# A decoder step whose mixture-of-experts loop takes experts 4 to 15 in an order worked out on the chip

## What is computed

```python
def moe_tokens(x, w_router, r_bias, wg, wu, wd):
    T = x.shape[0]
    scores = jax.nn.sigmoid(jnp.einsum('td,de->te', x, w_router, preferred_element_type=jnp.float32))
    ...
    h = jax.nn.silu(jnp.einsum('td,edf->tef', x, wg)) * jnp.einsum('td,edf->tef', x, wu)
    h = h * combine[..., None].astype(h.dtype)
    return jnp.einsum('tef,efd->td', h, wd)
```

## Time and profile before

| | us |
|---|---|
| median of 3 runs | 1412.61 (1407.36 to 1415.7) |
| the profiled execution | 1414.74 |
| its span | 1413.1 |
| TensorE, matmuls | 1206.3 busy, 85% of the span |
| VectorE | 463.3, 33% |
| ScalarE | 259.4, 18% |
| GpSimd | 157.0, 11% |
| chain that ended last | PE 68%, DMA 13%, DVE 10%, issue 4% |

### The profile page before, as it was taken

How to read it: one execution, slowest core, us unless ns; L and a number is a source line. 1 busy time by engine, 2 the same in 40 slices (tenths; PEclk the granted TensorE clock), 3 DMA queues, 4 the chain that set the end, 5 groups by cost and what they waited for, 6 DMA issues and landing times.

```text
span 1413.1 us, 26886 instructions
## 1 busy us (share of the span) xinstructions
PE 1206.3 (85%) x10864; PEld 784.3 (56%) x10865; DVE 463.3 (33%) x1207; ACT 259.4 (18%) x540; POOL 157.0 (11%) x249
## 2 busy tenths in 40 slices
PE   6998788999989899867997998999898789968950
PEld 4676555677747655433554676767567345424520
DVE  0025546412422423321434005132414333322435
ACT  0004631211311311100111212022203111101111
POOL 2005991000000000000001100000000000000022
PEclk9999998999999899988999897899998899989975
DMA  9646779833683779999959231134767697999530
GB/s 325 233 145 207 234 249 375 305 119 119 239 318 132 294 300 421 422 427 425 423 210 328 90 119 64 60 119 154 271 231 283 247 405 291 402 427 424 224 111 33
DMA packets 89226, 360.46 MB, mean 255 GB/s; under 512 B 7111, under 2 KB 7127, under 8 KB 72762
## 3 DMA queue, kind: packets, MB, share of 16 engines
q1 hardware_dynamic: 80418, 331.50, 61.0%
q0 software_dynamic: 8592, 27.68, 5.6%
q10 hardware_dynamic: 144, 0.26, 0.1%
HBM read 341.47 MB, written 18.38 MB: 255 GB/s over the span
## 4 chain that ended last, share of the span: by engine, by line
PE 68%; DMA 13%; DVE 10%; issue 4%; ACT 2%; SPq 1%; POOL 0%; DVEq 0%; POOLq 0%; ACTq 0%
PE acc L723 41%; PE psS L723 12%; PE psV L723 6%; DMA ring<-in_w_exp_up 4%; DMA by_slot<-arena 3%; DMA arena<-in_w_exp_gate 2%; DVE acts L1451 2%; PE acc L1015 2%; PE acc L826 1%; DMA ring<-in_w_in_even 1%; PE psN L1119 1%; DMA arena<-by_slot,arena 1%; PE acc L1149 1%; DVE arena L1808 1%; DVE arena L1834 1%
## 5 line engine op out<-in xcount | busy, mean ns | idle before, releaser
L723 PE MATMUL acc<-acts,ring 128*128 128x288 f32 x1280 | 318.9, 412 | 6.3 <-DMA ring<-in_w_in_even 3.6
L723 PEld LDWEIGHTS acc<-acts,ring 128*128 128x128 f32 x1280 | 246.9, 193 | 77.3 <-issue 5.4
L723 PE MATMUL psS<-arena,acts 128*32 128x256 f32 x1248 | 119.9, 415 | 16.9 <-issue 16.3
L723 PE MATMUL psS<-ring,acts 128*32 128x256 f32 x1728 | 110.7, 412 | 24.7 <-DMA ring<-in_w_exp_up 16.4
L1808 DVE COPY arena<-psV 32x256 f32<-32x256 f32 x208 | 87.3, 419 | 124.3 <-DMA by_slot<-arena 83.6
L723 PE MATMUL acc<-arena,acts 128*32 128x256 f32 (+4 forms) x1392 | 109.3, 392 | 7.6 <-DVE acts L1772 6.5
L723 PEld LDWEIGHTS psS<-ring,acts 128*32 128x32 f32 x1728 | 57.7, 118 | 76.1 <-issue 30.2
L1326 ACT ACTIVATE arena<-acc 128x1024 f32<-128x1024 f32 (+7 forms) x98 | 71.9, 758 | 111.3 <-PE acc L723 35.2
L1799 DVE TENSOR_TENSOR acts<-acts,psS 64x256 f32<-64x256 f32 x52 | 22.1, 425 | 207.2 <-ACT acts L2063 207.0
L723 PEld LDWEIGHTS psS<-arena,acts 128*32 128x32 f32 x1248 | 57.1, 118 | 54.8 <-issue 35.3
L2181 POOL DMA_DIRECT2D by_slot<-arena x52 | 25.7, 494 | 552.7 <-DVE arena L1808 552.7
(11 more groups left out here) (322 smaller groups left out, 1322.5 us busy)
## 6 DMA issues: line engine op xcount, KB each, us to landing
ring<-in_w_exp_gate SPq DMA_DIRECT2D x17, 2048.0 KB, 13.3
ring<-in_w_exp_up SPq DMA_DIRECT2D x17, 2048.0 KB, 17.2
ring<-in_w_exp_down SPq DMA_DIRECT2D x17, 2048.0 KB, 16.0
acts<-in_w_exp_down SPq DMA_DIRECT2D x10, 2048.0 KB, 16.3
arena<-in_w_exp_gate SPq DMA_DIRECT2D x10, 2048.0 KB, 15.9
arena<-in_w_exp_up SPq DMA_DIRECT2D x10, 2048.0 KB, 19.3
ring<-in_cache_k SPq DMA_DIRECT2D x64, 256.0 KB, 3.1
ring<-in_cache_v SPq DMA_DIRECT2D x64, 256.0 KB, 3.1
```

What stands on the lines that cost most here:

```text
L723: return pe.matmul(out, lhsT, rhs, start=first, stop=last)
```

## The change

- **Order.** Places 0 to 3 are still experts 0 to 3 (`FIXED`). Of experts 4 to 15 the two with the fewest chunks (`LIGHT`) take places 4 and 5; the others follow with the most chunks first, ties by number. VectorE compares all pairs (`KEY`, `ABOVE`, `HEAVIER`), gives each expert its place (`PLACED`), sums the chunks ahead of it (`BASE`) and writes the step table and the expert's number by place (`ORDER`, `ORDERI`). SP waits for `steps_ready` behind the loads of experts 0 to 3 and reads each later expert's number from `ORDERI`.
- **First chunk.** Expert 0 is in place 0, so its rows are its ranks: `G` of chunk 0 comes from `R` and `MASK` directly, ahead of all the arithmetic. `pick(1)` follows the row numbers.
- **Two key tiles.** `mk1` 0 and 1 are computed in `expert(0, ...)`, behind `mark(to_mark, gate_up_used)` and ahead of the third fetch; ScalarE empties them after the loop. For that `to_split` moves from `acc` to `psS[:, 1]`.

```diff
+FIXED, LIGHT = 4, 2
...
-        if l + 1 < DEPTH:
-            t.append((f"mk{l + 1}", 0, "s"))
...
-            t.append((f"mk{l + 1}", 1, "s"))
+            t += [(f"mk{l + 1}", 0, "s"), (f"mk{l + 1}", 1, "s")]
...
-                            e, at = 4 + 3 * i + j // 3, u + 12 + j
+                            at = u + 12 + j
+                            if j % 3 == 0:
+                                e = sp.value_load(ORDERI[0:1, bass.ds(FIXED + 3 * i + j // 3, 1)], min_val=FIXED, max_val=NE - 1)
...
-                experts_in(0, True, 4)
+                experts_in(0, True, FIXED)
+                sp.wait_ge(steps_ready, l + 1)
...
-                if l + 1 < DEPTH:
-                    memory_keys(l + 1, (0,))
...
+                    if e == 0 and l + 1 < DEPTH:
+                        memory_keys(l + 1, (0, 1))
...
-                to_split, to_turn, to_mark = (acc[:, spare_bank(l, n), :] for n in range(3))
+                to_split, to_turn, to_mark = psS[:, 1, :], acc[:, spare_bank(l, 0), :], acc[:, spare_bank(l, 1), :]
...
-                if l + 1 < DEPTH:
-                    memory_keys(l + 1, (1,))
...
+                S = chunks[l]
+                seq = cst[:, C_SEQ:C_SEQ + CAP].unsqueeze(1).to_broadcast([P, 3, CAP])
+                dve.tensor_tensor(PAIR[:, 0:3, :], R[:, 0:48].rearrange("p (t e) -> p t e", t=3)[:, :, 0:1].to_broadcast([P, 3, CAP]),
+                                  seq, ALU.is_equal).then_inc(S.match, 1)
+                dve.wait_ge(S.match, 1)
+                dve.tensor_tensor(G, PAIR[:, 0:3, :], MASK[:, :, 0:1].to_broadcast([P, 3, CAP]), ALU.mult).then_inc(S.picked, 1)
...
-                link(dve.tensor_tensor_scan(SCAN, ones[:, 0:NE], MORE, 0.0, ALU.mult, ALU.add))
-                link(dve.tensor_tensor(SCAN, SCAN, MORE, ALU.subtract))
-                link(dve.scalar_tensor_tensor(out=BASE, in0=SCAN, scalar=float(CAP), in1=cst[:, C_PLACE:C_PLACE + NE],
-                                              op0=ALU.mult, op1=ALU.add))
-                dve.tensor_tensor(POS, R[:, 0:48].rearrange("p (t e) -> p t e", t=3),
-                                  BASE.unsqueeze(1).to_broadcast([P, 3, NE]), ALU.add).then_inc(emptied["v"], 1)
+                many = NE - FIXED
+                link(dve.scalar_tensor_tensor(out=KEY, in0=MORE, scalar=float(CAP * NE), in1=cst[:, C_PLACE:C_PLACE + NE],
+                                              op0=ALU.mult, op1=ALU.subtract))
+                link(dve.tensor_tensor(ABOVE, KEY[:, FIXED:].unsqueeze(1).to_broadcast([P, many, many]),
+                                       KEY[:, FIXED:].unsqueeze(2).to_broadcast([P, many, many]), ALU.is_gt))
+                link(dve.tensor_reduce(HEAVIER, ABOVE, X, ALU.add))
+                dve.tensor_copy(PLACED[:, 0:FIXED], cst[:, C_SEQ:C_SEQ + FIXED])
+                link(dve.tensor_scalar(LAST_TWO, HEAVIER, many - LIGHT - 0.5, -float(many), ALU.is_gt, ALU.mult))
+                dve.tensor_scalar(EACH, MORE, 1.0, None, ALU.add)
+                link(dve.scalar_tensor_tensor(out=PLACED[:, FIXED:], in0=HEAVIER, scalar=float(FIXED + LIGHT), in1=LAST_TWO,
+                                              op0=ALU.add, op1=ALU.add))
+                link(dve.tensor_tensor(SQUARE, PLACED.unsqueeze(1).to_broadcast([P, NE, NE]),
+                                       PLACED.unsqueeze(2).to_broadcast([P, NE, NE]), ALU.is_lt))
+                link(dve.tensor_tensor(SQUARE, SQUARE, EACH.unsqueeze(1).to_broadcast([P, NE, NE]), ALU.mult))
+                link(dve.tensor_reduce(BASE, SQUARE, X, ALU.add))
+                dve.scalar_tensor_tensor(out=POS, in0=BASE.unsqueeze(1).to_broadcast([P, 3, NE]), scalar=float(CAP),
+                                         in1=R[:, 0:48].rearrange("p (t e) -> p t e", t=3), op0=ALU.mult, op1=ALU.add)\
+                    .then_inc(emptied["v"], 1)
...
-                dve.tensor_copy(SLOTNO, cst[:, C_SEQ:C_SEQ + CAP])
+                dve.tensor_scalar(SLOTNO, cst[:, C_SEQ:C_SEQ + CAP], float(CAP), None, ALU.add).then_inc(S.seq, 1)
...
-                S = chunks[l]
-                def pick(c, later):
-                    if later:
-                        dve.wait_ge(S.seq, c)
+                def pick(c):
+                    dve.wait_ge(S.seq, c)
...
-                    if later:
-                        dve.wait_ge(S.fetched, c)
+                    dve.wait_ge(S.fetched, c)
...
-                pick(0, False)
-                link(dve.tensor_copy(STEPS.rearrange("p (e j) -> p e j", j=2)[:, :, 0], MORE))
-                link(dve.tensor_scalar(STEPS.rearrange("p (e j) -> p e j", j=2)[:, :, 1], BASE, 1.0 / CAP, None, ALU.mult))
-                link(dve.tensor_tensor(LASTF, MORE[:, NE - 1:NE], STEPS[:, 2 * NE - 1:2 * NE], ALU.add))
+                pick(1)
+                pairs = STEPS.rearrange("p (e j) -> p e j", j=2)
+                link(dve.tensor_tensor(SLOT_OF, PLACED.unsqueeze(1).to_broadcast([P, NE, NE]),
+                                       cst[:, C_SEQ:C_SEQ + NE].unsqueeze(2).to_broadcast([P, NE, NE]), ALU.is_equal))
+                for n, what in enumerate((MORE, BASE, cst[:, C_SEQ:C_SEQ + NE])):
+                    link(dve.tensor_tensor(SQUARE, SLOT_OF, what.unsqueeze(1).to_broadcast([P, NE, NE]), ALU.mult))
+                    link(dve.tensor_reduce(pairs[:, :, n] if n < 2 else ORDER, SQUARE, X, ALU.add))
+                link(dve.tensor_tensor(LASTF, STEPS[:, 2 * NE - 2:2 * NE - 1], STEPS[:, 2 * NE - 1:2 * NE], ALU.add))
...
+                dve.tensor_copy(ORDERI, ORDER)
...
-                pick(1, True)
...
-                pick(2, True)
+                pick(2)
...
-                pick(3, True)
+                pick(3)
...
-                    pick(c + 3, True)
+                    pick(c + 3)
...
-                if l + 1 < DEPTH:
-                    memory_keys(l + 1, (0,))
...
-                    act.activation(XR, acc[:, spare_bank(l, 0), 0:256], ACT.Copy).then_inc(S.split, 1)
+                    act.activation(XR, psS[:, 1, 0:256], ACT.Copy).then_inc(S.split, 1)
...
-                                   acc[:, spare_bank(l, 1), 0:256].rearrange("p (j q m) -> p j q m", j=2, q=4), ACT.Copy)\
+                                   acc[:, spare_bank(l, 0), 0:256].rearrange("p (j q m) -> p j q m", j=2, q=4), ACT.Copy)\
...
-                if l + 1 < DEPTH:
-                    memory_keys(l + 1, (1,))
...
-                    memory_keys(l + 1, (2, 3))
+                    memory_keys(l + 1, (0, 1, 2, 3))
...
```

More of the change, by code:

```diff
@@ L359, in build @@
         BASE = view(11728, NE)
-        SCAN = view(11744, NE)
+        EACH = view(11744, NE)
         ROW = view(11760, 2, 3)
@@ L374, in build @@
         SLOTNO = view(12464, CAP)
+        KEY, PLACED = view(12496, NE), view(12512, NE)
+        HEAVIER, LAST_TWO = view(12528, NE - FIXED), view(12544, NE - FIXED)
+        ORDER, ORDERI = view(12560, NE), arena[:, 12576:12576 + NE].bitcast(I32)
+        SQUARE = view(11264, NE, NE)
+        SLOT_OF = acts[:, 2 * UNIT + 1248:2 * UNIT + 1504].rearrange("p (a b) -> p a b", b=NE)
+        ABOVE = view(11264, NE - FIXED, NE - FIXED)
         RT = arena[:, 12128:12128 + 672]
```

## The result

| | before | changed |
|---|---|---|
| median of 12 runs, us | 1415.56 (1407.36 to 1419.64) | 1407.59 (1401.83 to 1412.64) |
| profiled execution, us | 1414.74 | 1401.83 |
| TensorE busy, share of the span | 85% | 86% |
| chain that ended last | PE 68%, DMA 13%, DVE 10%, issue 4% | PE 69%, DMA 11%, DVE 9%, issue 5%, SPq 3% |

What follows compares the result with a forecast made beforehand. Each expert loop was taken as bound by weight loads in one part and by TensorE in the other. Layer 0's -9.2 and layer 1's -18.1 sum to -27.3 from 1414.74, 1387.4 us; forecast 1387, range 1372 to 1403.

Steps and rivals of the forecast that it cites:

- G(6): Start of the gate-up matmuls for the first chunk of the expert in place 6; forecast 573.9 us in layer 0.
- G(10): Start of the first chunk's gate-up matmuls in place 10; forecast 662.5 us in layer 0, 1274.4 in layer 1.
- G(15): Start of the first chunk's gate-up matmuls in place 15; forecast 718.6 us in layer 0, 1330.5 in layer 1.
- (a): Head of layer 0: without the key tile as filler the router runs at lower clock, rank result 1.7 us later.
- (b): Heads of both layers: first pick needs two instructions behind the rank, 0.56 us against 3.05, a gain of 2.5.
- my rivals: Four alternatives: faster still (10%), slower loads in the tail (8%), the lead is lost (6%), order not as read (4%).
- Rival 2: Tail loads at 5.34 us per matrix and four code stalls, +17 us: 1404, or 1402 from the median; 8%.
- (c): Head of layer 0: both key tiles, 7.14 us each, behind the first mark; tiles until 511.1, loads resume at 511.2.
- s = +7.9: Layer 0: shift in us of everything behind the second key tile, whose end moves from 503.24 to 511.1.
- Places 4 to 10: Layer 0 loop: TensorE's pace, 11 chunks of 8.05 us from place 6 to 10, loads always three experts ahead.
- The tail, G(15) = G(10) + 56.1: End of both loops: place 12 issued 1.1 us before G(10), then 2 us plus 11 matrices of 5.02, continuously.
- One code stall in layer 1: Layer 1, place 6: a loop-body copy's first extra chunk stalls TensorE at issue, 3.2 us taken once.

Runs made afterwards that it cites:

- wait_late: Changed kernel with TensorE's wait for the rank bank moved behind the second fetch; median 1400.8 us, ratio 0.9907 to the kernel before.
- tiles_only: Kernel before with only the two memory key tiles moved behind the first chunk's mark; median 1425.7 us, ratio 1.0087 to the kernel before.
- best_spread: `best` with experts 4 to 15 taken light and heavy by turns; median 1370.8 us, ratio 0.9691 to the kernel before.
- order_only: Kernel before with only the new order of experts 4 to 15, old first pick and old tile places; median 1395.4 us, ratio 0.9875.
- pick_late: Kernel before with only the direct first pick and the rank-bank wait behind the second fetch; median 1411.7 us, ratio 0.9983.
- best: Changed kernel with the key tiles at their old places and the rank-bank wait behind the second fetch; median 1388.7 us, ratio 0.9808 to the kernel before.

## Why the prediction was wrong, point by point

The direction and the order's mechanism were right, the size was not. Forecast and measured starts in layer 0 (layer 1 behind its rank result, 1094.55 in the forecast and 1091.63 measured):

| | forecast | measured | off |
|---|---|---|---|
| rank result, layer 0 | 482.0 | 481.27 | -0.7 |
| `turn_h` | 496.35 | 500.10 | +3.8 |
| end of the second key tile | 511.1 | 516.8 | +5.7 |
| G(6) | 573.9 | 580.53 | +6.6 |
| G(10) | 662.5 | 669.23 | +6.7 |
| G(15) | 718.6 | 728.67 | +10.1 |
| last down | 728.6 | 739.61 | +11.0 |
| layer 1: G(10) | 179.9 | 184.5 | +4.6 |
| layer 1: G(15) | 236.0 | 244.0 | +8.0 |
| layer 1: last down | 246.0 | 253.6 | +7.6 |

- *(a) Router at half clock: right.* Granted clock 0.50, 7.95 us. I took the rank result 1.7 us later from layer 1; behind the variance tile it was 1.2 later (23.17 us from that tile's start, 21.98 before).
- *(b) First pick, a gain of 2.5 in both layers: this step failed.* "The first pick needs two instructions behind the rank" is true of VectorE and says nothing of who uses it. I listed what stands ahead of `turn_h` on VectorE's queue, and not what stands ahead of the fetch on TensorE's: a wait for `POS`, which the change itself had made later. The fetch came 4.39 us behind the rank result, not 0.7. `wait_late` puts that at 3.4 to 4.7 us a layer, 8.1 in all. None of my rivals held it. Rival 2's 1404 lies near the measured 1407.6, but not for its reasons: the tail's matrices came at 5.04 us each, not 5.34, and TensorE's stalls at "issue" near the heads of the loops are three as before (1.89, 1.99 and 2.88 us, before 2.25, 2.15 and 2.61).
- *(c) Two tiles behind the first mark, s = +7.9: right in kind, 1.5 short.* The two tiles take 15.6 to 15.7 us, not 14.2: they start behind a head in which TensorE stood idle, part of them ran below full clock (0.79 from 500 to 508 us), and the 7.14 came from a tile in a busy stretch. `tiles_only` costs 9.4 from the rank on; without the direct pick and the later rank my working gives 8.7 for it (7.9 + 2.5 - 1.7). I had seen that the removed filler costs the router its clock and did not apply it to the tiles. SP's load resumed right behind them, as forecast, at 516.87.
- *Places 4 to 10: right.* From G(6) to G(10) 88.7 us for 11 chunks, 8.06 each (8.05 forecast), and no wait for a load there.
- *The tail, G(15) = G(10) + 56.1: short by 3.3 us in layer 0 and 3.4 in layer 1.* In layer 0 place 12's gate was issued 1.2 us before G(10), as forecast, and the rate was right: from its landing to that of place 15's up matrix it took 50.4 us for ten matrices, 5.04 each. The start was mis-sized. Three loads, issued at 659.18 (place 11's down matrix), 668.01 (place 12's gate) and 694.11 (place 15's up matrix), with the us from issue to landing last:

```profile
acts<-in_w_exp_down SPq DMA_DIRECT2D x1, 2048.0 KB, 12.4
...
ring<-in_w_exp_gate SPq DMA_DIRECT2D x1, 2048.0 KB, 10.2
...
ring<-in_w_exp_up SPq DMA_DIRECT2D x1, 2048.0 KB, 34.5
```

I allowed 2 + 5.02 us for the second, as on an empty queue; it took 10.2. The queue was not empty: the down matrix landed at 671.6, 3.6 us behind that issue. TensorE's waits in the tail end at most 0.1 us behind the landings of three up matrices (698.3, 713.4, 728.6), also the two that the profile puts down to "issue". In layer 1 the loads were not continuous either. Place 10 has two chunks there, which my list of the new order says and my sum left out: place 13's gate was issued only 15.4 us behind G(10), and it landed 6.5 us behind the matrix before it instead of 5.0, which is 1.5 of the 3.4; place 12's gate took 8.4 from its issue instead of 7.0, which is 1.4. As for the rate, DMA moved 415 GB/s from 668 to 740 us. By the Trainium skill, "DMA: Bandwidth & Descriptors", section "Where 436 GB/s comes from", the HBM side of about 358 would bind; no saturated stretch here shows that. The Trainium skill's "HBM Reference", section "Specifications (TRN2)", says that a core that streams alone gets about 425; the trace agrees with that one (427 at 675 to 700 in `best_spread`).
- *One code stall in layer 1, 3.2 us, in place 6: one came, but not there.* TensorE stood 2.88 us at "issue" at 1154.56, inside place 4's first gate-up, which took 8.66 us instead of 3.66. Before, the stall is in the same gate-up (2.61 at 1155.43). Place 4 now has one chunk, and where a copy now runs its first extra chunks, in place 6, nothing of the kind is seen. So it does not hang on the extra chunk, as I had read it; its cause stays open.
- *What the order is worth.* Before, the five long intervals of layer 0 between down projections (11.8, 16.0, 14.5, 16.1, 14.2) are 32 us above five chunks of 8.1. In `order_only` three are left (15.1, 14.4, 16.1), 21 us above. That removes 11, and the later head (its first down projection stands 2.9 us later behind the rank) takes 2.9 back, which comes near the 8.4 measured. The new order did not remove the waits; a third of them is gone, and the rest stands in the tail.

The miss is 18.6 us in the sum of both layers (-8.7 at the two last downs against -27.3): the wait 8.1, the tails 6.7, the tiles 1.5, less 0.7 for the rank result. Some 3 us are left. Single rows that my sum did not have are layer 1's second gate-up with its fetch (8.56 us instead of 5.30 before, the clock's fall seen in `pick_late`), the stall in place 4 (5.0 us in that gate-up instead of 3.2) and place 15's gate-up in layer 0 (6.46 instead of 5.55). They make more than 3; some intervals behind them were shorter than forecast, and the balance was not followed further. With the wait moved and the tiles left alone, the measured gain (`best`, ratio 0.9808) is the 27 us of the forecast, by other terms than mine, so that agreement is luck. That the profiled execution lay 12.9 us and not 8 under its counterpart is the last section's matter.

## What to carry to other kernels

When a result is made earlier on one engine, read the consumer's queue up to the instruction that uses it: every wait there must be early too, above all one whose signaller the same edit moved later. Work that fills a gap on TensorE can keep the clock up for what follows: with the tile moved out, the router took 7.95 us instead of 4.25. The price of the moved work is its time at its new place, 15.7 us here and not 14.2. Where loads and matmuls bind by turns, alternate light and heavy experts rather than sort them: with a ring of three places neither a run of light ones nor a full ring behind a heavy one may last long.

## What the runs showed that I had not expected

The same code ran at different clocks from execution to execution, far from the change. Between the two expert loops, behind the same wait of 1.09 us, the same 48 matmuls took 7.84 us in the changed kernel and 13.75 in `best`:

```profile
875.24 7.84 PE L731 MATMUL acc<-arena 128*128 128x128 f32 x48 [1.09 <-ACT arena L1332]
```

```profile
865.28 13.75 PE L733 MATMUL acc<-arena 128*128 128x128 f32 x48 [1.09 <-ACT arena L1336]
```

The granted clock from 860 to 900 us was 0.70 before, 0.87 in the changed kernel and 0.66 in `wait_late`, though the last two differ by one line elsewhere. From the last down projection of layer 0 to the router of layer 1 the eleven kernels without the filler take between 335.2 us (`pick_late`) and 345.4 (`best`), in no order that follows their edits. That is as large as the effect studied: a single profile of `wait_late` (1403.49) stands above that of the changed kernel (1401.83), while its median is 6.8 us lower. What decides the clock in a given execution was not tried.
